# Moving the second-to-last expert pair's down projection behind the last pair's gate and up projections

## The reference

```python
for e in range(N_EXPERTS):                       # 16 experts, hidden 512
    hid = jax.nn.silu(t @ w_g[e]) * (t @ w_u[e])  # gate and up, 2048 -> 512
    y = y + comb[:, e:e + 1] * (hid @ w_d[e])     # down, 512 -> 2048
...
xp = xp + ga2c * y                                # gate vector, residual
y_prompt = _rmsnorm(xp, final_norm_g)             # over all 2048 columns
```

## Time and profile before

| | |
|---|---|
| median of 3 runs | 1286.12 us (1283.91 to 1287.06) |
| the profiled execution's own time | 1286.12 us |
| its span, first to last instruction | 1283.4 us |
| TensorE busy | 1159.9 us, 90% of the span |
| VectorE busy | 510.8 us, 40% |
| ScalarE busy | 374.7 us, 29% |
| DMA, mean over the span | 334 GB/s |
| DMA from slice 27 of 40 on, all but the last two | 401 to 422 GB/s |

### The profile page before, as it was taken

How to read it: one execution, slowest core, us unless ns; L and a number is a source line. 1 busy time by engine, 2 the same in 40 slices (tenths; PEclk the granted TensorE clock), 3 DMA queues, 4 the chain that set the end, 5 groups by cost and what they waited for, 6 DMA issues and landing times.

```text
span 1283.4 us, 14178 instructions
## 1 busy us (share of the span) xinstructions
PE 1159.9 (90%) x5573; PEld 689.6 (54%) x5573; DVE 510.8 (40%) x722; ACT 374.7 (29%) x531; POOL 43.5 (3%) x79
## 2 busy tenths in 40 slices
PE   4678899999999999999999998999898888988784
PEld 1135566767766667767887785444343333423231
DVE  0122455545543435545565545124233232404035
ACT  3212534433342333334445535121011011201013
POOL 0020000010000200000000000000000000000000
PEclk9779899999999999999999998999999999999987
DMA  9999898798865988888575437999999999999998
GB/s 379 407 355 384 293 342 306 274 333 296 283 245 181 339 309 322 304 320 279 186 249 187 165 132 282 401 421 421 422 421 422 421 421 422 421 421 421 421 408 337
DMA packets 104433, 428.41 MB, mean 334 GB/s; under 512 B 8760, under 2 KB 8936, under 8 KB 70960
## 3 DMA queue, kind: packets, MB, share of 16 engines
q1 hardware_dynamic: 99808, 415.26, 84.1%
q0 software_dynamic: 4112, 12.19, 3.1%
q10 hardware_dynamic: 448, 0.07, 0.0%
HBM read 423.53 MB, written 3.95 MB: 333 GB/s over the span
## 4 chain that ended last, share of the span: by engine, by line
PE 68%; DMA 26%; DVE 2%; issue 1%; SPq 1%; ACT 1%; DVEq 0%; POOL 0%; ACTq 0%
PE bank L682 14%; PE bank L684 13%; PE bank L683 13%; PE bank L1042 10%; DMA mraw<-in_w_exp_up 8%; DMA raw<-in_w_ada 7%; DMA mraw<-in_w_exp_gate 5%; DMA mraw<-in_w_exp_down 5%; PE bank L664 5%; PE bank L1072 3%; PE bank L983 2%; DMA cst<-in_cache_v_ctx 1%; PE bank L648 1%; PE bank L828 1%; PE bank L1093 1%
## 5 line engine op out<-in xcount | busy, mean ns | idle before, releaser
L1546 DVE TENSOR_TENSOR w_lo<-raw,w_hi 128x1024 fp32r<-128x1024 f32 x192 | 234.1, 1225 | 278.6 <-ACT w_hi L1202 277.9
L1202 ACT ACTIVATE w_hi<-raw 128x1024 fp32r<-128x1024 f32 x192 | 202.6, 1059 | 319.5 <-PE bank L684 240.1
L1042 PE MATMUL bank<-mraw,xg 128*64 128x512 f32 x1024 | 233.6, 600 | 23.3 <-DMA mraw<-in_w_exp_gate 13.5
L682 PE MATMUL bank<-w_hi,h_hi 128*128 128x512 f32 x512 | 210.7, 412 | 3.9 <-DVE w_lo L1546 3.9
L684 PE MATMUL bank<-w_hi,h_lo 128*128 128x512 f32 x512 | 201.3, 393 | 0.0
L683 PE MATMUL bank<-w_lo,h_hi 128*128 128x512 f32 x512 | 201.0, 393 | 0.0
L1042 PEld LDWEIGHTS bank<-mraw,xg 128*64 128x64 f32 x1024 | 76.6, 137 | 156.2 <-issue 154.7
L1072 PE MATMUL bank<-mraw,hidT 128*64 128x512 f32 x448 | 101.4, 596 | 26.2 <-DMA mraw<-in_w_exp_down 26.2
L682 PEld LDWEIGHTS bank<-w_hi,h_hi 128*128 128x128 f32 x512 | 97.3, 190 | 49.9 <-issue 30.8
L684 PEld LDWEIGHTS bank<-w_hi,h_lo 128*128 128x128 f32 x512 | 97.0, 190 | 21.4
L683 PEld LDWEIGHTS bank<-w_lo,h_hi 128*128 128x128 f32 x512 | 97.4, 190 | 19.4 <-issue 1.0
(11 more groups left out here) (251 smaller groups left out, 1065.4 us busy)
## 6 DMA issues: line engine op xcount, KB each, us to landing
mraw<-in_w_exp_gate SPq DMA_DIRECT2D x68, 1024.0 KB, 13.5
mraw<-in_w_exp_up SPq DMA_DIRECT2D x68, 1024.0 KB, 13.6
raw<-in_w_in SPq DMA_DIRECT2D x64, 1024.0 KB, 5.9
raw<-in_w_ada SPq DMA_DIRECT2D x64, 1024.0 KB, 7.6
mraw<-in_w_exp_down SPq DMA_DIRECT2D x64, 1024.0 KB, 13.6
raw<-in_w_ada SPq DMA_DIRECT2D x64, 512.0 KB, 8.6
raw<-in_w_out SPq DMA_DIRECT2D x16, 1024.0 KB, 5.0
raw<-in_w_na_o SPq DMA_DIRECT2D x8, 1024.0 KB, 5.1
```

The lines of the kernel that those rows point to most:

```text
L682: nc.tensor.matmul(o, hi[:, k, s], wh, start=k == 0, stop=False)
L1042: last = nc.tensor.matmul(out[x * CAP:(x + 1) * CAP], xg[:, q * LOAD_K + kk, e * CAP:(e + 1) * CAP], mraw[:, slot, kk * COL:(kk + 1) * COL ...
L1202: nc.scalar.activation(w_hi[:, u % AHEAD], r, ACT.Copy).then_inc(hi_ready, 1)
L1546: v.tensor_tensor(w_lo[:, u % AHEAD], r, w_hi[:, u % AHEAD].bitcast(F32), ALU.subtract).then_inc(raw_done[n % RAW], 4)
```

## The change

The order of the last 16 units changes for loads and for TensorE. Before: gate/up of pair 7 (q 0 and 1, 4 units), down of pair 6 (4), gate/up of pair 7 (q 2 and 3, 4), down of pair 7 (4). After: gate/up of pair 7 (8 units), down of pair 6 (4), down of pair 7 (4). The four scatters of pair 6, which stood between the gate/up units of pair 7, now stand in twos behind `down_half(0)` and `down_half(1)`. `silu` and `hidden` of pair 7 move ahead of the output work of pair 6 on ScalarE and VectorE. `load_sqrt_table` is no longer called in the loop. On VectorE, `key` and `build_pick` move behind `final_gain(1)`.

```diff
         def gate_up_unit(i, q, up):
             ...
-            return 12 * i - 4 + n + (4 if n >= 4 else 0)
+            return 12 * i - 4 + n + (4 if i < PAIRS - 1 and n >= 4 else 0)
         def down_unit(i, k):
-            return 12 * i + 12 + k - (4 if i == PAIRS - 1 else 0)
+            if i >= PAIRS - 2:
+                return 88 + 4 * (i - PAIRS + 2) + k
+            return 12 * i + 12 + k
 # SyncE
-                for i in range(1, PAIRS):
+                for i in range(1, PAIRS - 1):
...
+                for q in range(4):
+                    for up in range(2):
+                        gate_up_loads(r, PAIRS - 1, q, up)
+                down_loads(r, PAIRS - 2)
                 last_down_loads(r)
 # TensorE
-                for i in range(1, PAIRS):
+                for i in range(1, PAIRS - 1):
                     gate_up(i, 0, 0)
...
+                for q in range(4):
+                    for up in range(2):
+                        gate_up(PAIRS - 1, q, up)
+                    if q == 0:
+                        hidden_transposes(PAIRS - 2)
+                down(PAIRS - 2, 0)
+                down(PAIRS - 2, 1)
                 hidden_transposes(PAIRS - 1)
+                down(PAIRS - 2, 2)
+                down(PAIRS - 2, 3)
                 down_half(0)
+                scatter(PAIRS - 2, 0)
+                scatter(PAIRS - 2, 1)
                 down_half(1)
+                scatter(PAIRS - 2, 2)
+                scatter(PAIRS - 2, 3)
                 down_half(2)
                 scatter(PAIRS - 1, 0)
                 scatter(PAIRS - 1, 1)
 # ScalarE
+                    if i == PAIRS - 1:
+                        silu(i)
+                        hidden(i)
                     next_group(i, 0)
                     outputs_high(i - 1)
                     next_group(i, 4)
-                silu(PAIRS - 1)
-                load_sqrt_table()
-                hidden(PAIRS - 1)
                 outputs_high(PAIRS - 1)
 # VectorE
                 def last_outputs():
                     i = PAIRS - 1
-                    dve.wait_ge(pick_ready, r * 2 + 2)
-                    v.tensor_scalar(key[:], key[:], -float(CAP), None, ALU.add).then_inc(key_moved, 1)
-                    dve.wait_ge(key_moved, r + 1)
-                    build_pick(0, EPG)
                     output_low(i, 0)
                     output_low(i, 1)
                     add(i, 0)
                     add(i, 1)
                     final_gain(0)
                     final_gain(1)
+                    dve.wait_ge(pick_ready, r * 2 + 2)
+                    v.tensor_scalar(key[:], key[:], -float(CAP), None, ALU.add).then_inc(key_moved, 1)
+                    dve.wait_ge(key_moved, r + 1)
+                    build_pick(0, EPG)
                     output_low(i, 2)
...
                     hidden(i - 1)
+                    if i == PAIRS - 1:
+                        hidden(i)
...
-                hidden(PAIRS - 1)
                 last_outputs()
```

## The result

The changed kernel takes 1293.81 us in the median of six runs (1291.33 to 1296.77), the kernel before 1286.59 us in its six. The two medians are 7.2 us apart. The ratio, which isn't taken from the two medians (nine executions of the changed kernel are on record, up to 1300.92 us), is 1.0067, with a 95% interval from 1.0044 to 1.009: 8.6 us slower, between 5.7 and 11.6. I had forecast 4.94 us and 1291.1 us. The direction was right and the loss too small: the median of 1293.81 us lies inside my range of 1287.0 to 1294.4, but the ratio on 1286.12 us gives 1294.7 us, just above it.

The account below looks back on a forecast made before the run. Loads were taken to bound the expert stage, with what runs behind the last landings deciding the end. 2.87 + 0.91 + 0.27 + 0.89 = 4.94 us on 1286.12 gave 1291.1 us, range 1287.0 to 1294.4.

Parts of the forecast that it names:

- What the change can win: TensorE's two losses around `down_half(0)` in the kernel before: 4.5 us late start plus 3.1 us at low clock, 7.6 us.
- the prediction's own bound by landings: If landings alone held TensorE, `scatter(7, 0)` would start at 1252.1 instead of 1256.51 and the time be 1283.8 us.
- Loads bound the stage, and both orders move the same: Expert stage: both orders move 96 equal units, one every 4.97 us, so the last lands at the same time.
- `down_half(0)` 4.5 us earlier and at full clock: `down_half(0)` starts with its landing at 1238.62, at 2.4 GHz, taking 3.58 us instead of 6.66.
- Four scatters, two stalls: Pair 6's scatters in twos cost TensorE 4.1 us, plus 5.4 us for two stalls waiting on adds.
- The step that failed: TensorE's schedule behind each stall: scatter 1.02 us, next `down_half` 3.59 us; `scatter(7, 0)` 2.87 us later than before.
- the clock falls in the stalls: Rival: TensorE's idling 2.6 us twice lowers its clock, next step takes 3.1 us more, 1294.2 us; chance 0.10.
- `key` and `pick`: On VectorE, between the gain products and `d_lo` of block 2, where VectorE doesn't pause: +0.91 us.
- The table load: The tail's root on ScalarE needs a square-root table load, starting as the last square's sum is read: +0.89 us.
- A drain with the table load: Rival: a drain adds 1.38 us between table load and root in the tail, giving 1292.5 us; chance 0.02.
- Clock of the last scatters: TensorE idles 4.4 us before `scatter(7, 2)`, so the clock has most likely fallen at its start: +0.27 us.
- The other side: Rival: adds never hold up a scatter, `scatter(7, 0)` comes 3.0 us early, 1285.1 us; chance 0.16 for 1285 to 1289.

Follow-up runs that it names:

- e5_hid_first: Kernel before with one move: on VectorE `hidden(7)` stands ahead of `add(6, 3)` instead of behind it; ratio 0.9973 to the kernel before.
- e2_spread: Changed kernel with pair 6's four scatters one by one, behind `down(6, 3)` and `down_half(0)` to `down_half(2)`; ratio 1.0036 to the kernel before.
- e3_cover: Changed kernel with `load_sqrt_table()` back behind `silu(7)` and `key`/`build_pick` back behind `hidden(7)`; ratio to the kernel before 1.0075, then 1.0054 when run again.
- e1_fill: Changed kernel with ten unused matmuls in each of TensorE's two waits between scatters of pair 6; ratio 1.0043 to the kernel before.
- e4_uncover: Kernel before with only `key` and `pick` moved behind `final_gain(1)` and the dummy square root (table load) removed; ratio 1.0006 to the kernel before.
- e8_repaired: Changed kernel's unit order with scatters spread, `down_half(3)` ahead of `scatter(7, 0)`, `key`/`pick` and table load covered; ratio 1.0014 to the kernel before.
- e7_fill_before: Kernel before with 14 unused matmuls in TensorE's wait for the last hidden values; ratio 0.9984 to the kernel before.

## Why the prediction was wrong in size, point by point

- *What the change can win*, 7.6 us: too large. It adds up TensorE's two losses, but the last landings stop the gain before that: e5_hid_first won 3.9 at `scatter(7, 0)`, and the prediction's own bound by landings is 4.4. The forecast isn't touched, since its schedule has no such term.
- *Loads bound the stage, and both orders move the same.* Right: `down_half(0)` landed 20.00 us after the start of unit 88, 0.11 later than by my rhythm (1238.62 - 1218.73 = 19.89).
- *`down_half(0)` 4.5 us earlier and at full clock.* Right: it took 3.59 us to the scatter.
- *Four scatters, two stalls.* Right in place and length: 3.76 us from scatter to scatter, forecast 3.74. Shown by e2_spread too, where they are gone.
- *The step that failed*: "`down_half(1)` +1.02 = 1246.97, `scatter(6, 2)` +3.59", and the same for `down_half(2)`, at full clock. The scatters behind the stalls took 2.01 and 1.84 us instead of 1.02, the steps behind them 4.27 and 4.45 instead of 3.59: 3.35 us. Of these 0.47 were covered, since VectorE held `scatter(7, 0)` that much behind TensorE in my schedule (1259.38 against 1258.91); with the 0.11 of the landing and 0.04 of the two stalls the 2.87 became 5.90. It was the rival "the clock falls in the stalls", to which I had given 0.10 and a price of 3.1, for one slow step. That this price is near the 3.35 is luck: each stall cost 1.67, there were two, and in the second execution they cost 4.9 together. Its argument against, a gap of 2.1 us that had kept 1.00, was one gap in another stage; here the clock fell in or behind stalls of 2.57 us, twice in each of four executions with them (two of the changed kernel, two of e3_cover). That idleness is the cause, and not the neighbouring work, is shown by e1_fill.
- *`key` and `pick`*, 0.91: measured 0.90. *The table load*, 0.89: measured 0.93. The load started at 1288.39, before the value that its root waits for was made (L1576, from 1288.55), so it lies ahead of the wait, as I had it.
- *A drain with the table load*: the root starts 0.01 us behind the load's end, so the 1.38 us of the Trainium skill ("ScalarE: Activation LUTs", What ACT_TABLE_LOAD costs) don't appear here; its 1283 ns for the load agree with 1.28.
- *Clock of the last scatters*, +0.27: wrong in sign in the first profile (-0.42), where the clock was still up after 4.40 us of idleness; in the second, and in e1_fill and e4_uncover, it had fallen after 4.4 us, as forecast.
- *The other side* ("the stalls aren't there"): even without them, in e2_spread and e8_repaired, the order isn't faster. That rival overlooked the adds of pair 6 on VectorE, behind which `scatter(7, 0)` waits in e2_spread. It counted TensorE alone.
- With the clock's term at 3.35 in place of 0, less 0.47 for VectorE, and the last scatters at -0.42, the sum is 7.3 us, the measured tail. The times give 8.6 (5.7 to 11.6) and 9.1 us in the two comparisons. Whether the average execution loses nearer 7.3 or 9.7 us is open: two profiles show two values for the clock's part.

## What to carry to other kernels

Work that is moved from beside a bound stream to behind its last landing must be counted on every engine: here TensorE started its last pair earlier, and paid with stalls between the scatters and with adds of VectorE that then held it. Before reordering a whole pair, look for the single late instruction: one move on VectorE won 4.2 us where the reordering lost 7.3. And when a wait like these of 2.57 us comes into a dense stretch of TensorE, count the work behind it at the low clock as a real case, and read in several executions what it costs.

## What the runs showed of the hardware

- The granted clock fell in, or up to some 1.6 us behind, idle stretches of 2.57 us between scatters and matmuls, and stayed at 0.50 for 3.4 to 6.8 us. Ahead of `scatter(7, 2)`, after 4.4 us of idleness, it was still at 1.00 in one execution and down in three; after 3.53 us it stayed at 1.00 through the scatters in both of e3_cover, fell in the midst of them in the kernel before and in e5_hid_first, and was down at their start in e7_fill_before.
- Ten or fourteen matmuls with no use, put into a wait, made the kernel's end come sooner: 2.0 us in e1_fill, 2.6 in e7_fill_before.
- Loads for a round that never runs delayed the output's transfers: 9.1 us from their issue to the end of the span with them in the way (1285.0 - 1275.87), 7.0 without (1276.3 - 1269.28).
- The start of unit 88, behind nearly the same work, varied by 11 us between profiled executions, more than everything that this change did. The length of an execution went with its granted clock: of the nine of the changed kernel, the three longest (1297.88 to 1300.92 us) had a mean of 0.962 to 0.963, the other six (1291.33 to 1296.77) of 0.968 to 0.972. In which stretch ahead of unit 88 the time goes isn't shown. Only times counted from a landmark behind the common part could be compared.
